# Four seven-product groups, in place of three and a plain product, in the down projections of the plain gated layers

## What is computed

```python
def swiglu(x, w_gate, w_up, w_down):
    return (jax.nn.silu(x @ w_gate) * (x @ w_up)) @ w_down
# first block, twice:
x = x + 0.5 * rmsnorm(swiglu(rmsnorm(x, g1), w1_gate, w1_up, w1_down), g1_post)   # D_FF = 2816
x = x + rmsnorm(mixers(rmsnorm(x, g)) @ w_out, g_post)                            # attention, convolution
x = x + 0.5 * rmsnorm(swiglu(rmsnorm(x, g2), w2_gate, w2_up, w2_down), g2_post)   # D_FF = 2816
x = x + rmsnorm(sigmoid(rmsnorm(x, g) @ w_ple_gate) * (p @ w_ple_proj), g_post)
# second block, once: a mixer, then a gated layer with a convolution and GELU, D_FF_2 = 3072, then an embedding layer
```

## Time and profile before

| | us |
|---|---|
| median of 3 runs | 2737.08 (2735.86 to 2737.13) |
| the profiled execution | 2738.14 |
| its span, first to last instruction | 2736.3 |
| PE busy in the span | 2726.7 |
| DVE busy in the span | 2058.2 |
| ACT busy in the span | 1624.2 |

### The profile page before, as it was taken

One profiled execution on the slowest core, in us unless ns is written; L12 is line 12 of the kernel. 1 busy time (PEld: TensorE's weight loads), 2 busy tenths in 40 slices (PEclk: granted clock), 3 DMA queues, 4 the chain that ended last, 5 costly groups with the idle time before them and its releaser, 6 DMA issues.

```text
span 2736.3 us, 46133 instructions
## 1 busy us (share of the span) xinstructions
PE 2726.7 (100%) x18546; PEld 2488.2 (91%) x18546; DVE 2058.2 (75%) x2754; ACT 1624.2 (59%) x2519; POOL 142.4 (5%) x160
## 2 busy tenths in 40 slices
PE   9999999999999999999999999999999999999999
PEld 8999987599999999999976799999987889999998
DVE  7878766767687787787757587787876746989868
ACT  6556644565566685565636565566754546666665
POOL 0000000000000000000000000000001100000000
PEclk9999999999999999999999999999999999999999
DMA  7776623037776327775331247765232323777651
GB/s 221 179 199 172 177 57 100 18 100 186 190 212 161 106 82 206 177 216 155 93 92 49 93 133 177 206 165 168 78 97 92 93 77 101 182 195 202 153 179 55
DMA packets 177139, 382.55 MB, mean 140 GB/s; under 512 B 35616, under 2 KB 80032, under 8 KB 176928
## 3 DMA queue, kind: packets, MB, share of 16 engines
q1 hardware_dynamic: 159216, 315.63, 37.0%
q0 software_dynamic: 17568, 63.97, 13.6%
q10 hardware_dynamic: 144, 0.00, 0.0%
HBM read 364.87 MB, written 12.58 MB: 138 GB/s over the span
## 4 chain that ended last, share of the span: by engine, by line
PE 99%; DVE 0%; ACT 0%; DMA 0%; issue 0%; SPq 0%; DVEq 0%; ACTq 0%
PE banks L742 31%; PE banks L743 31%; PE banks L744 31%; PE banks L1292 1%; PE banks L1314 1%; PE banks L1351 1%; PE banks L1303 1%; PE banks L1355 0%; PE banks L1341 0%; PE banks L781 0%; PE banks L1445 0%; DVE PT L3180 0%; PE banks L1274 0%; PE banks L1238 0%; PE banks L1187 0%; PE banks L1276 0%
## 5 line engine op out<-in xcount | busy, mean ns | idle before, releaser
L742 PE MATMUL banks<-HH,WH 128*128 128x256 f32 (+1 forms) x3244 | 1015.7, 313 | 2.0 <-ACT R L1697 1.9
L743 PE MATMUL banks<-HH,WL 128*128 128x256 f32 (+1 forms) x3244 | 1010.9, 312 | 0.0
L744 PE MATMUL banks<-HL,WH 128*128 128x256 f32 (+1 forms) x3244 | 1010.6, 312 | 0.0
L742 PEld LDWEIGHTS banks<-HH,WH 128*128 128x128 f32 x3244 | 619.1, 191 | 44.8 <-issue 8.0
L743 PEld LDWEIGHTS banks<-HH,WL 128*128 128x128 f32 x3244 | 619.2, 191 | 34.8 <-issue 1.0
L744 PEld LDWEIGHTS banks<-HL,WH 128*128 128x128 f32 x3244 | 619.1, 191 | 34.1
L588 DVE TENSOR_TENSOR WL<-raw,WH 128x1024 fp32r<-128x1024 f32 (+1 forms) x308 | 370.7, 1205 | 215.7 <-ACT WH L583 214.9
L583 ACT ACTIVATE WH<-raw 128x1024 fp32r<-128x1024 f32 (+1 forms) x308 | 319.4, 1040 | 291.8 <-DVE raw L2528 120.5
L742 PE MATMUL banks<-SH,WH 128*128 128x256 f32 x1472 | 416.6, 283 | 0.0
L743 PE MATMUL banks<-SH,WL 128*128 128x256 f32 x1472 | 416.6, 283 | 0.0
L744 PE MATMUL banks<-SL,WH 128*128 128x256 f32 x1472 | 416.6, 283 | 0.0
(11 more groups left out here) (341 smaller groups left out, 3670.2 us busy)
## 6 DMA issues: line engine op xcount, KB each, us to landing
extra_raw<-in_w_quarters SPq DMA_DIRECT2D x96, 512.0 KB, 4.5
raw<-in_w_quarters SPq DMA_DIRECT2D x48, 512.0 KB, 5.0
raw<-in_w_in SPq DMA_DIRECT2D x46, 512.0 KB, 3.7
spare_raw<-in_w_quarters SPq DMA_DIRECT2D x36, 512.0 KB, 4.2
extra_raw<-in_w_quarters POOLq DMA_DIRECT2D x36, 512.0 KB, 7.3
raw<-in_w_down SPq DMA_DIRECT2D x30, 512.0 KB, 3.7
extra_raw<-in_last_quarters SPq DMA_DIRECT2D x26, 512.0 KB, 4.4
raw<-in_w_quarters POOLq DMA_DIRECT2D x24, 512.0 KB, 6.3
```

The source lines that it names most:

```text
L742: e.matmul(o, wh, ah, start=start, stop=False, skip_group_check=skip)
L743: e.matmul(o, wl, ah, start=False, stop=False, skip_group_check=skip)
L744: return e.matmul(o, wh, al, start=False, stop=stop, skip_group_check=skip)
```

## The change

In stages 0, 2, 4 and 6 (`four_down`) the early rows are one unit (hidden rows 8 and 9) in place of four. Rows 10 to 15 go into that half of the output by a new group n+3, whose seven products leave out the first of four row pairs (`first = 1`): six trios in each phase, not eight. Group n+3 uses the row sums of rows 8 to 15 again. DVE adds it onto the early banks, as it adds group n (`vector_add`), and the seeds are made while group n+3 runs; rows 16 to 21 begin with the seeded banks and not with the early ones. ACT and DVE get new orders for these groups, SP loads five quarters more and three units less and fetches the parked sums at other places, POOL issues two loads more. In stage 9, ACT's `hidden_high` and DVE's `hidden_low` of row 16 move behind the split of the second plain unit. The diff, with context lines left out and the functions that dispatch:

```diff
...
+def four_down(s):
+    return s < 9
+def early_units(s):
+    return 1 if four_down(s) else 4
 def seven_groups(s):
-    return range(2, gated_groups(s) + 3)
+    return range(2, gated_groups(s) + 3 + four_down(s))
+def down_groups(s):
+    return range(gated_groups(s), gated_groups(s) + 3 + four_down(s))
 def down_half(s, g):
...
-    return n % 2 if g == n else 1 - n % 2
+    return n % 2 if g in (n, n + 3) else 1 - n % 2
...
-        for kp in range(4):
+        for kp in range(early_units(s)):
...
-        for g in seven_groups(s)[-3:]:
+        for g in down_groups(s):
...
         def place(s, g, t, m):
-            return two((R, RP)[t]) if g == gated_groups(s) + 2 else quadrant(t, m)
+            n = gated_groups(s)
+            if g < n + 2:
+                return quadrant(t, m)
+            return two((R, RP)[t]) if m else C[:, t, 0, :].rearrange("p (c t) -> p c t", c=2)
         def quarter_out(s, g, t, m):
...
-                e.wait_ge(*pe.at("unit", W[s, "seven", seven_groups(s)[-1 - (tile_of[u] == NSPLIT + 1)], 6]))
+                g = gated_groups(s) + 1 if tile_of[u] == NSPLIT + 1 else seven_groups(s)[-1]
+                e.wait_ge(*pe.at("unit", W[s, "seven", g, 6]))
...
-                           *(((s, 11, "b11"), (s, 11, "b22")) if n > 11 else (W[s, "early", 0], W[s, "early", 2])))
+                           *(((s, 11, "b11"), (s, 11, "b22")) if n > 11 else (W[s, "early", 0], (s, 11, "sum"))))
...
-                if key == (s, n + 2, "b21"):
+                if key == ((s, n + 3, "b11") if four_down(s) else (s, n + 2, "b21")):
...
-                if key == W[s, "down", DOWN_WHOLE]:
+                third, fourth = ((s, n + 3, "sum"), (s, n + 3, "b22")) if four_down(s) else (W[s, "down", DOWN_WHOLE],) * 2
+                if key == third:
...
+                if key == fourth:
...
         def sync_between(e, u):
...
-            return (b[3], b[1], b[2]) if g == n + 1 else tuple(b[:3])
+            return (b[3], b[1], b[2]) if g in (n + 1, n + 3) else tuple(b[:3])
         def seven_free(s, g):
...
-            first = [vec.at("evacuated", s, (n - 1) % 2, 3)] if g == n + 1 else [act.at("c21", s, n)]
-            return [first, [act.at("c11", s, g - 1)], [vec.at("c12", s, g - 1)]]
+            first = [vec.at("evacuated", s, (n - 1) % 2, 3)] if g == n + 1 else [act.at("c21", s, g - 2)]
+            second = [vec.at("half_added", s, 0, 0)] if g == n + 3 else [act.at("c11", s, g - 1)]
+            return [first, second, [vec.at("c12", s, g - 1)]]
         def row_sums(tile, i):
...
-            late = g == gated_groups(s) + 2
+            late = g > gated_groups(s) + 1
...
+            first = 1 if g == gated_groups(s) + 3 else 0
             def chunk(j, t):
...
-                    for kp in range(4):
+                    for kp in range(first, 4):
...
-                                    opens and up == kp == 0, kp == 3, not (opens and up == 0))
+                                    opens and up == 0 and kp == first, kp == 3, not (opens and up == 0))
...
         def tensor_ffn(e, s):
...
-            for g in seven_groups(s)[-3:]:
+            for g in down_groups(s):
...
-            added = [[vec.at("quarter_added", s, t, m) for t in range(2)] for m in range(2)]
+            last = n_groups + 3 if four_down(s) else n_groups
+            added = [[vec.at("quarter_added", s, last, t, m) for t in range(2)] for m in range(2)]
...
-                             early + late[2:] + late[:2], False)
+                             late + early if four_down(s) else early + late[2:] + late[:2], False)
         def tensor_early_rows(e, s):
...
-            for kp in range(4):
+            for kp in range(early_units(s)):
...
-        def scalar_seed(e, s, i):
+        def scalar_seed(e, s, i, *waits):
...
-            e.wait_ge(*act.at("c21", s, n + 1))
+            for wait in waits:
+                e.wait_ge(*wait)
...
         def scalar_ffn(e, s):
...
+        def scalar_short_rows(e, s):
+            n = gated_groups(s)
+            scalar_c21(e, s, n - 1)
+            scalar_hidden_high(e, s, 4)
+            scalar_hidden_high(e, s, 6)
+            scalar_row_sum_high(e, s, 0)
+            split_high(e, W[s, "seven", n, 2])
+            scalar_row_sum_high(e, s, 1)
+            for k in range(1, DOWN_SEVEN, 2):
+                scalar_hidden_high(e, s, k)
         def scalar_down_seven(e, s, g):
...
-                u2_free, u3_free, c11_free = ([vec.at("quarter_added", s, t, m)] for t, m in ((0, 1), (1, 1), (0, 0)))
+                u2_free, u3_free, c11_free = ([vec.at("quarter_added", s, n, t, m)] for t, m in ((0, 1), (1, 1), (0, 0)))
...
-                            vec.at("quarter_added", s, 1, 0))
+                            vec.at("quarter_added", s, n, 1, 0))
...
+            if four_down(s) and g == n:
+                scalar_silu_half(e, s, n - 1, 1)
+                scalar_row_sum_high(e, s, 2)
...
+            if four_down(s) and g == n:
+                scalar_row_sum_high(e, s, 3)
...
-            split_high(e, after_seven(s, g, 0))
-            scalar_copy(e, s, g, "u3", 4, x, place(s, g, 1, 1), *u3_free)
-            if g == n + 2:
-                scalar_hidden_high(e, s, DOWN_WHOLE)
+            if four_down(s) and g == n:
+                scalar_copy(e, s, g, "u3", 4, x, place(s, g, 1, 1), *u3_free)
+                split_high(e, after_seven(s, g, 0))
+            else:
+                split_high(e, after_seven(s, g, 0))
+                scalar_copy(e, s, g, "u3", 4, x, place(s, g, 1, 1), *u3_free)
...
+            if four_down(s) and g == n:
+                for k in (10, 12, 14):
+                    scalar_hidden_high(e, s, k)
...
-            if g < n + 2:
+                if four_down(s):
+                    for k in (11, 13, 15):
+                        scalar_hidden_high(e, s, k)
+            if four_down(s) or g < n + 2:
...
+            scalar_hidden_high(e, s, DOWN_WHOLE)
...
-                scalar_seed(e, s, i)
+                scalar_seed(e, s, i, act.at("c21", s, n + 1))
+        def scalar_last_down_seven(e, s, g):
+            x, y, z = seven_banks(s, g)
+            split_high(e, W[s, "seven", g, 3])
+            scalar_copy(e, s, g, "p1", 0, x, third(y), seven_free(s, g)[1][0])
+            split_high(e, W[s, "seven", g, 4])
+            scalar_seed(e, s, 0)
+            scalar_copy(e, s, g, "q5", 1, z, Q5C[:], vec.at("c22", s, g - 1))
+            split_high(e, W[s, "seven", g, 5])
+            scalar_copy(e, s, g, "u2", 2, x, place(s, g, 0, 1), vec.at("half_added", s, 0, 1))
+            split_high(e, W[s, "seven", g, 6])
+            scalar_copy(e, s, g, "c11", 3, y, place(s, g, 0, 0), act.at("seed", s, 0))
+            split_high(e, W[s, "down", DOWN_WHOLE])
+            scalar_copy(e, s, g, "u3", 4, x, place(s, g, 1, 1), vec.at("half_added", s, 1, 1))
+            scalar_hidden_high(e, s, DOWN_WHOLE)
+            scalar_seed(e, s, 1, act.at("c11", s, g))
+            split_high(e, W[s, "down", DOWN_WHOLE + 1])
+            scalar_seed(e, s, 2, vec.at("c12", s, g))
+            scalar_copy(e, s, g, "c21", 6, x, place(s, g, 1, 0), act.at("seed", s, 1))
+            scalar_seed(e, s, 3, act.at("c21", s, g))
+            scalar_hidden_high(e, s, DOWN_WHOLE + 1)
         def scalar_late_sum_high(e, s, i):
...
+                    if four_down(s):
+                        vector_row_sum(e, s, 2)
...
-                    vector_hidden_low(e, s, 10)
-                    vector_hidden_low(e, s, 11)
+                    for k in (0, 2) if four_down(s) else (10, 11):
+                        vector_hidden_low(e, s, k)
...
+        def vector_short_rows(e, s):
+            n = gated_groups(s)
+            vector_half_scale(e, s, n - 1, 1)
+            vector_weight_sum(e, s, n, 2)
+            vector_hidden_low(e, s, 4)
+            vector_hidden_low(e, s, 6)
+            split_low(e, W[s, "seven", n, 2])
+            vector_row_sum_low(e, s, 0)
+            vector_row_sum(e, s, 3)
+            vector_row_sum_low(e, s, 1)
+        def vector_first_of_four(e, s, g):
+            split_low(e, W[s, "seven", g, 3])
+            for k in range(1, DOWN_SEVEN, 2):
+                vector_hidden_low(e, s, k)
+            split_low(e, W[s, "seven", g, 4])
+            vector_half_hidden(e, s, g - 1, 1)
+            vector_row_sum_low(e, s, 2)
+            split_low(e, W[s, "seven", g, 5])
+            vector_row_sum_low(e, s, 3)
+            vector_weight_sum(e, s, g, 6)
+            split_low(e, W[s, "seven", g, 6])
+            split_low(e, W[s, "seven", g + 1, 0])
+            split_low(e, W[s, "seven", g + 1, 1])
+            vector_c22(e, s, g)
+            vector_weight_sum(e, s, g + 1, 2)
+            vector_c12(e, s, g)
+            split_low(e, W[s, "seven", g + 1, 2])
         def vector_first_down_seven(e, s, g):
...
-            e.tensor_tensor(rows, rows, quadrant(t, m), ALU.add).then_inc(*vec.done(("quarter_added", s, t, m)))
```

(96 more changed lines are left out.)

11 lines of the change are left out of this document (5 added, 6 removed).

## The result

The changed kernel takes 2743.36 us (median of 9 runs, 2741.97 to 2746.68) where the kernel before takes 2736.18 (9 runs, 2735.35 to 2740.0): ratio 1.0028, 95% interval 1.0019 to 1.0037. It is slower by 7.2 us, and outside the range; the forecast was 2734.5. The profiled execution took 2742.68 us with a span of 2740.9.

The account below looks back on a forecast made before the run. PE bound the kernel, busy 2726.7 of 2736.3 us. Matmuls -4.9, front and tail 4 x (0.25 + 0.25), stage 9 +0.35: -2.55 us, so 2734.5 against the median; own range 2733 to 2736.5, 8-in-10 range 2731.6 to 2741.

Parts of the forecast that it names:

- I take 0: Group 14's phase 4 weights: added quarter ready at 315.8, ACT asks at 316.5, so no cost; bounds nothing to 3.3 late.
- Cost 0: Groups 12 and 13: moved splits and later fetches cost nothing; every deadline checked keeps 1.5 us or more.
- the sum: All terms: -4.9 + 4 x (0.25 + 0.25) + 0.35 = -2.55 us, giving 2734.5 against the median.
- The walk: New engine orders stepped through stage 0 from old times and median landings, to check that PE's needs are ready in time.
- The tail: End of group 14 into row 16: DVE's addition for bank 4 late, 0.25 us a stage; bounds nothing or 1 us.
- rival 1: Last group's added quarter lands late, each late us costing PE one; +0.2% at 2.0 us late; chance 0.12 beyond that.
- rival 4: ACT's or DVE's queue slips 0.5 to 1 us at front and tail: 2738.5; chance 0.16, shared with rival 1 below 2.0 us.
- the 17.7 us of stage 9: Stage 9, group 14, before: time from issue until ACT could go on for the same kind of quarter; PE then waited 2.03.
- 1.22 us a stage: Matmul gain: 72 wide ones lost (16.34 us), 126 narrow ones gained (15.12 us); 4.9 us in four stages.
- rival 3: Narrow matmuls cost less than 0.120 us beyond the columns: up to 1.93 us a stage, 2729.4; chance 0.03.
- The lag at the front: Group 11, phases 1, 4 and 6: DVE's row sums late by some 0.2 us, paid once; 0.25 us a stage taken.
- Stage 9: Row 16's hidden_low 0.65 us late, less 0.3 from a seed wait that goes: 0.35 us lost (0 to 0.7).

Follow-up runs that it names:

- e2: Changed kernel without the adding loads of groups 11 to 14 in stages 0, 2, 4 and 6, their sums left out; 2733.59 us, ratio 0.9991 to the kernel before.
- e10: Changed kernel with third quarter and parked-sum-1 fetch earlier, group 14's DVE and ACT tail reordered, and no adding loads in groups 11 to 14; 2733.94 us.
- after: The changed kernel as first measured, with all its adding loads, beside the kernel before; 2743.36 us, ratio 1.0028.
- e8: Changed kernel without the two adding loads of group 14 alone (8 transfers over four stages), their sums left out; 2736.85 us, ratio 1.0002 to the kernel before.
- e7: Control: the kernel before, without the adding loads of groups 11 to 13 in stages 0, 2, 4 and 6; 2735.94 us, ratio 0.9998.
- e11: Changed kernel without the two adding loads of group 13 alone, group 14's staying; 2743.19 us, ratio 1.0027 to the kernel before.
- e3: Changed kernel with SP issuing the quarter 'third' before b21 in groups 11 to 14 of the four stages; 2738.97 us, ratio 1.001 to the kernel before.
- e4: Changed kernel with DVE's order at the end of group 14 changed: c12 first, row 17's weight split last; 2739.16 us, ratio 1.0011 to the kernel before.

## Why the prediction was wrong

*What failed: the loads.* "I take 0" for the added quarter of group 14, and "Cost 0" for groups 12 and 13. With those transfers out of the way the change measures -2.5 us (e2) and -2.7 (e10), against -2.55 in the sum. So the other terms, taken together, were about right; this one was 9.8 us in size (e2 against after), 6.5 of them by group 14's adding loads alone (e8). That the sum agrees to a tenth is partly luck: in e2 PE lost 2.5 us ahead of row 16 in the four stages where I had 1.0, in row 16 0.75 for 1.0, and in stage 9 nothing for 0.35.

In stage 0 the sizes compare step by step. The walk had the quarter ready 0.7 us before ACT asked for it; it was 1.55 late, 2.3 us worse:
- Weight sum 6 of group 13, behind which it is issued, ended 6.8 us before group 14's first matmul, in the walk 8.5: 1.7 us. This was the largest piece. Without adding loads DVE kept the walk to a tenth (9.7 us ahead at its start, walked 9.7). So the walk of DVE was right and its inputs late: ACT stood for transfers of 1.97, 1.75 and 2.42 us before, all of which I had put at nothing.
- From issue to ready 11.7 us for 10.6: 1.15 us. It is the adding load's, 7.2 us for 6.0; up to POOL's issue it took 4.55 for the 4.6 of the walk. I had taken medians of a stretch of before; in after the median of the adding loads is 7.3, not 6.0, and that of the fetches 6.9, not 3.8. SP now issues nine loads and fetches from 263.5 to 275.0.
- ACT itself asked 0.6 us later than walked, which gives that much back.

*Groups 12 and 13.* "Every deadline I checked keeps 1.5 us or more" had no late load in it. In stage 2 PE itself lost 0.71 and 0.96 us in groups 12 and 13, and 0.48 more at group 14's phase 4. The second of them in the weight loads' timeline:

```profile
875.88 0.19 PEld L760 LDWEIGHTS banks<-HH,WH 128*128 128x128 f32 x1 [0.97 <-DVE WL L604]
```

*The tail.* I took 0.25 us; in after it is 1.1 at row 16 in stages 0, 2 and 4, 0.7 in stage 6, and 0.6 for the copy in all but stage 6. But in e2 it is one wait of 0.34 on the weight loads, at bank 4 and for the addition that was named. Its price by the matmuls' starts is 0.19 us. The size was right for transfers in time. The place where an order without slack meets a late transfer was seen as rival 1's price ("every us late is a us of PE"), and that price is about right, rather too low: 1.55, 2.02, 1.96 and 0.49 us late in the four stages, and 2.2, 2.7, 2.8 and 0.9 us lost at phase 4, the copy and row 16, 8.5 in all, where the price and my 0.25 a stage give 7.0. The lateness is 1.5 us on average, less than the 2.0 from which rival 1 decided; the rest of the 11.7 us is 1.9 in groups 12 and 13, nearly all of it in stage 2, and 1.3 at the front. The mechanism was rival 1; it had a chance of 0.12, and a part of rival 4's 0.16 below it. What spoke for it was in view: the 17.7 us of stage 9. I set that aside because fetches are over by then; they are, but their delay had gone into ACT and DVE.

*What held.* The narrow matmuls are 0.120 us apart, so the arithmetic of 1.22 us a stage stands, and rival 3 falls. By the Trainium skill (TensorE: Matmul & The Clock Gate, Back-to-back issue gap) the change would have gained 1.8 us a stage or lost; neither gap shows here. PE timeline after, group 14:

```profile
298.04 0.28 PE L761 MATMUL banks<-HIDH_HIGH,WL 128*128 128x256 f32 x1
298.16 0.28 PE L762 MATMUL banks<-HIDL_LOW,WH 128*128 128x256 f32 x1
298.28 0.28 PE L760 MATMUL banks<-HIDH_HIGH,WH 128*128 128x256 f32 x1
```

The lag at the front was about 0.25 us in stage 0, as forecast, at two of the three phases named. Where it is longest, in stage 4, the trace names DVE's row sum as forecast. PE timeline after:

```profile
1231.44 0.36 PE L760 MATMUL banks<-HH,WH 128*128 128x256 f32 x1 [0.23 <-DVE HL L2685]
```

*Stage 9.* +0.35 was forecast; no wait is there in after. And the 2.03 us wait, which I called unchanged, is in no other profile of this study, nor is it in e7's, which leaves stage 9 as it was. It belonged to that execution. The step from the profiled execution to the median took off 1.06 us, where the waits of stage 9 alone were 2.3.

*Left open.* Why DVE is 1.7 us late with group 13's adding loads gone (e11) as well as with them; whether group 12's load or the fetch does it. The adding loads of groups 11 and 12 and the new places of the fetches were never undone alone on the changed kernel. And e3, e4 and the copy's place were not timed each with all the others in place, so their shares (4.4 and 4.2 alone, 7.2 together) aren't a sum.

## What to carry to other kernels

Before taking plain work out from under a stage, list each transfer that this work covered and redo its landing with the longest time of the new stretch, counting that an in-order engine which waits once issues its next load later: here waits of 2 us on ACT, which cost PE hardly anything where they stood in stage 0, went with DVE 1.7 us behind and the last load late. A walk from medians finds the right order of events and no lateness; where the chain behind a load has no slack, price the late case first. To see if transfers are the cause, leave them out in the changed kernel and in the one before: what it moves in each (here 9.8 and 0.3 us) is the answer. Part of the loss (4.2 us, e4) came back by order alone, which gave the chain slack.

## What the runs showed of the hardware

- An adding load of 512 KB took 5.8 / 7.3 / 8.9 us to land (shortest, median, longest; 200 to 320 us of after), a plain one 3.5 / 4.8 / 7.7 in the same stretch. A fetch of parked sums took 6.5 / 6.9 / 9.4, longer than a plain load of weights; in the same stretch of before, where the four fetches were spread over 11.5 us with three loads between them (five in after), 3.7 / 3.8 / 6.7.
- The times of after scatter by 4.7 us between runs, those without its adding loads by 2.1 (e2), those of before without them by 0.9 (e7). But the nine runs of before beside after scatter by 4.7 us too, and there no transfer held PE up in these stages, so a wide scatter is no sign of a late transfer.
- Leaving out the 24 adding loads of the four stages' down groups from the kernel before moved its time by 0.3 us, within the noise: PE wasn't measurably slowed by these transfers beside it, only by waiting for them in the changed kernel.
